# A planner's urge count started at one: context blocks behind every block of x from the first layer on

## What is computed

```python
x = first_block(x, ...)      # layer 0: pool + gated mixer, FFN; layer 1: NSA attention + retention, FFN
h, hc = x, ctx
for i in range(2):           # second_block; ctx_out is true for i = 0 alone
    m, mc = adaln(c, ada_w[i], ada_b[i]), adaln(c_ctx, ada_w[i], ada_b[i])
    h  = half_ffn(h,  m,  0, ..., ffn_w_in[i, 0], ffn_w_out[i, 0])
    hc = half_ffn(hc, mc, 0, ..., ffn_w_in[i, 0], ffn_w_out[i, 0])
    y, yc = mixer_i(modulated_norm(h), modulated_norm(hc), ...)  # i = 0: differential attention, i = 1: GQA
    h  = half_ffn(gated_residual(h, y), m, 6, ..., ffn_w_in[i, 1], ffn_w_out[i, 1])
    if ctx_out:
        hc = half_ffn(gated_residual(hc, yc), mc, 6, ...)
return h
```

## Time and profile before

| | us |
|---|---|
| median of 3 runs | 2725.43 |
| lowest, highest | 2722.52, 2730.79 |
| the profiled execution, its own time | 2730.84 |
| its span | 2729.1 |
| PE busy | 2536.8 (93%) |
| DVE busy | 1692.8 (62%) |
| ACT busy | 1246.3 (46%) |
| mean granted TensorE clock | 0.966 |
| loads | 480.11 MB, mean 176 GB/s |

### The profile page before, as it was taken

How to read it: one execution, slowest core, us unless ns; L and a number is a source line. 1 busy time by engine, 2 the same in 40 slices (tenths; PEclk the granted TensorE clock), 3 DMA queues, 4 the chain that set the end, 5 groups by cost and what they waited for, 6 DMA issues and landing times.

```text
span 2729.1 us, 48500 instructions
## 1 busy us (share of the span) xinstructions
PE 2536.8 (93%) x20604; PEld 2410.3 (88%) x20604; DVE 1692.8 (62%) x2817; ACT 1246.3 (46%) x1697; POOL 1.2 (0%) x6
## 2 busy tenths in 40 slices
PE   6799997999999999999898998999999999887998
PEld 5689986888998999999887998999999999766998
DVE  6565564656756655566767566577655557746655
ACT  4443452444544444445455454445444445435443
POOL 0000000000000000000000000000000000000000
PEclk9799999999999999999898999999999999888999
DMA  6456655523555665644351344554545545363453
GB/s 218 175 198 247 240 204 210 207 99 125 195 181 216 237 231 195 222 140 157 124 189 47 112 179 145 183 185 171 179 162 185 186 174 182 120 216 136 170 178 116
DMA packets 71590, 480.11 MB, mean 176 GB/s; under 512 B 8785, under 2 KB 9297, under 8 KB 17745
## 3 DMA queue, kind: packets, MB, share of 16 engines
q1 hardware_dynamic: 66240, 468.74, 48.1%
q10 hardware_dynamic: 5136, 8.28, 1.0%
HBM read 471.48 MB, written 1.05 MB: 173 GB/s over the span
## 4 chain that ended last, share of the span: by engine, by line
PE 75%; DVE 12%; ACT 6%; DMA 4%; issue 3%; ACTq 0%; DVEq 0%
PE bank L263 66%; ACT whi L222 3%; DMA raw<-w_main 2%; DVE wlo L242 2%; PE bank L1116 2%; DVE wlo L229 2%; PE bank L998 1%; PE bank L936 1%; DVE HX L638 1%; DVE ARX L687 1%; DVE tmpx L632 1%; DMA raw<-w_down 1%; PE bank L986 1%; PE bank L553 1%; PE bank L1640 0%
## 5 line engine op out<-in xcount | busy, mean ns | idle before, releaser
L263 PE MATMUL bank<-HNX_hi,whi 128*128 128x256 f32 x2968 | 865.9, 293 | 69.7 <-DVE wlo L242 28.3
L222 ACT ACTIVATE whi<-raw 128x2048 fp32r<-128x2048 f32 (+1 forms) x378 | 705.5, 1868 | 336.2 <-PE bank L263 168.2
L263 PE MATMUL bank<-HNX_hi,wlo 128*128 128x256 f32 x2968 | 849.6, 287 | 0.0
L263 PE MATMUL bank<-HNX_lo,whi 128*128 128x256 f32 x2968 | 835.2, 287 | 0.0
L229 DVE TENSOR_TENSOR wlo<-raw,whi 128x1024 fp32r<-128x1024 f32 (+1 forms) x378 | 453.5, 1200 | 575.1 <-ACT whi L222 574.6
L263 PEld LDWEIGHTS bank<-HNX_hi,whi 128*128 128x128 f32 x2968 | 582.0, 196 | 96.9 <-issue 52.0
L263 PEld LDWEIGHTS bank<-HNX_hi,wlo 128*128 128x128 f32 x2968 | 582.5, 196 | 0.0
L263 PEld LDWEIGHTS bank<-HNX_lo,whi 128*128 128x128 f32 x2968 | 574.0, 196 | 1.1 <-issue 0.9
L242 DVE TENSOR_TENSOR wlo<-raw,whi 128x1024 fp32r<-128x1024 f32 (+1 forms) x378 | 451.1, 1193 | 0.0
L263 PE MATMUL bank<-HNC_hi,whi 128*128 128x256 f32 x1344 | 389.0, 289 | 10.4 <-DVE HNC_lo L701 4.3
L263 PE MATMUL bank<-HNC_lo,whi 128*128 128x256 f32 x1344 | 380.7, 283 | 0.0
(11 more groups left out here) (341 smaller groups left out, 2945.4 us busy)
## 6 DMA issues: line engine op xcount, KB each, us to landing
raw<-w_main SPq DMA_DIRECT2D x270, 1024.0 KB, 4.8
raw<-w_ada SPq DMA_DIRECT2D x72, 1024.0 KB, 4.8
raw<-w_down SPq DMA_DIRECT2D x72, 1024.0 KB, 4.9
raw<-w_down SPq DMA_DIRECT2D x36, 768.0 KB, 4.2
raw<-w_cmp SPq DMA_DIRECT2D x4, 1024.0 KB, 5.1
tmpx<-ARX ACTq DMA_DIRECT2D x18, 128.0 KB, 4.6
tmpx<-ARX ACTq DMA_DIRECT2D x32, 64.0 KB, 4.7
HX<-x_in SPq DMA_DIRECT2D x2, 512.0 KB, 5.9
```

The source lines that it names most:

```text
L222: NS.activation(WHI[q % HIS][:, 0:size], RAW[m % SLOTS][:, 0:size], ACT.Copy).then_inc(sems["w_hi"], 1)
L263: return NT.matmul(dst, (WHI[ordinal[n] % HIS], WLO[n % SLOTS])[w][:, k * 2 * P + col:k * 2 * P + col + P], x[xp][:, kx, :], start=start, ...
```

## The change

One number: `urge[0]` starts at 1 instead of 0, so that `pace` may step c once before every half block of x from the start.

```diff
             lanes, ahead, paused = {}, {}, {"a"}
-            clock, ready_at, turns, urge = [0.0], {"c": 0.0, "a": 0.0}, [0], [0]
+            clock, ready_at, turns, urge = [0.0], {"c": 0.0, "a": 0.0}, [0], [1]
             DENSE, ADA = 2.9, 1.2
```

## The result

| | before | changed |
|---|---|---|
| median | 2723.97 us | 2776.08 us |
| lowest, highest | 2719.87, 2730.79 | 2773.81, 2779.39 |
| span of the profiled execution | 2729.1 | 2775.0 |
| mean granted TensorE clock | 0.966 | 0.955 |

The account below looks back on a forecast made before the run. PE, busy for 93% of the span, was taken as the bound, so only its own order could matter. Terms against the profiled execution summed to +5 us, 2736, or 2730 against the median of 2725.43; range 2706 to 2756.

Parts of the forecast that it names:

- The GQA: Keys and values of the GQA: x goes on earlier, c's two blocks and small steps only move; -11 us (-12 to -9).
- The norm before `gu2`: Five blocks of `da_in` become four of `da_out` with sums on DVE; 8 lost against 2.5, +6 us (0 to 11).
- `od_in`: Eight blocks of c spread over it: cover gains 4, the end of c's FFN costs 12; +8 us (-15 to +14).
- the differential attention: Nine units without a block for eight, the first three covered; +2 us (-3 to +6).
- the loop: NSA loop: 12 blocks of c for 18, units 0 to 4 bare, half of c's norm there; +8 us (3 to 15).
- Tail: NSA loop's end, tile norm to `od_out`: x's chain 17 us bare, taken as 22 with c's steps; +10 us (5 to 15).
- norm before `gu1`: From five blocks of c to none, with three of a and pieces of c's attention: 14 lost against 3.0, +11 (7 to 16).
- The norm before `gu4`: Two blocks of c for five, but these without sums or products on DVE; -2 us.
- `gu1` and `gu2`: The `gu1` term: 12 us of loss and small waits of about 3 leave, c's attention comes in; -13 us.
- Rival 1: More cover in `od_in` pays: that term becomes -22 for +8, giving 2700 us; chance 21%.
- Rival 2: NSA loop to `gu2`: lost cover costs full price, four terms 57 for 35, deciding past about 45; 2752 us, chance 24%.
- Rival 3: Lower clock in NSA's early units, its end and the norm, 0.74 instead of 1.00: +7, 2737 us; chance 11%.

Follow-up runs that it names:

- experiment 1: Kernel before, with the urge at 3 from x's `gu4` on, so c's two `ga_in` blocks and tile norm come earlier: 2710.12 us against 2726.52, ratio 0.9941.
- experiment 11: Kernel before, with the urge at 1 from the end of x's first FFN, so `od_in` has blocks of c without sums: 2744.19 us, ratio 1.0093.
- experiment 4: Kernel before, with c held during units 0 to 4 of the NSA loop: 2728.5 us, ratio 1.0008.
- experiment 7: Changed kernel, with the row of a finished ahead of the last two blocks of `od_in` instead of ahead of the NSA loop: 2772.92 us, ratio 1.0187.
- experiment 8: Changed kernel, with no row of a ahead of the NSA loop; a stops at a border of its rows: 2764.91 us, ratio 1.0159.
- experiment 10: Kernel before, with four blocks of a in a row ahead of its NSA loop, where it has one: 2734.63 us, ratio 1.0049.
- tail_bare: Kernel before, with c and a held from the end of the NSA loop to the norm (last of the 12 to 14 group): 2735.63 us, ratio 1.0048.
- experiment 3: Kernel before, with c held during x's norm before `gu1` alone: 2736.66 us, ratio 1.0034.
- experiment 6: Changed kernel, with the urge at 3 in x's `da_in` and back at 2 for the differential attention: 2768.94 us, ratio 1.0173.
- experiment 12: Changed kernel, with both c and a held from the end of the NSA loop to the end of the norm before `gu1`: 2763.0 us, ratio 1.0146.
- experiment 13: Kernel before, with c and a held during x's norm before `gu1` alone: 2730.86 us, ratio 1.0029.

## Why the prediction was wrong, step by step

**Right.** `gu0`, -1. The GQA, -13 for -11 (experiment 1). The norm before `gu2` and `da_in` within 4. `od_in`, +9 for +8, is right in what costs there, the end of c's FFN (experiment 11), and not in how: of its two parts the gain by cover was 2 and not 4, and the longest wait goes by ScalarE's order and not by VectorE's sums in a split. The five bare units cost 6 to 8 (experiment 4) for +8; that is partly luck, since the term had counted c's norm among them, and the run has no norm there.

With a's blocks and the small matmuls taken off, as in the prediction's norms, two terms broke out of their ranges most: the differential attention, +17 for +2 (upper end 6), and the loop, +18 for +8 (upper end 15). Tail and norm before `gu1`, +15 each, stand at or near their upper ends.

**"The three blocks of a ahead of it need no split and cost what they did."** This is the step that failed in kind. It counted them as PE work. In a row they empty the four buffers: 7 to 8 us in the loop (77.7 lost without their own work in the changed kernel, 69.7 and 71.0 when they stand elsewhere, experiments 7 and 8), 11 to 12 in the kernel before when put there (experiment 10). The prediction had reckoned with the four buffers in `od_in`, and did not ask the same of the loop's start. A second step failed in the same term: it took PE's work in the bare units at its covered price, 3.4 us for a unit. In the rows of the loop PE is idle for 12.7 us for 2.7, close to the term's 10 for 2, but 6.9 of them are the wait for the end of the row, which the term did not have. And PE's work itself got longer: its busy time, less 0.1195 for each matmul of a block and less a's 2.8, is 65.1 us for 56.4, at a granted clock of 0.90 for 0.99. So the loop's 21 are 10 of idle time, 9 of slower small matmuls and 3 of a's work.

**The tail**, +22 for +10 (upper end 15). x's bare chain was sized well: 18.3 us in the run `tail_bare` (VectorE's timeline, 663.33 to 681.59) for 17. With its guests it takes 25.4 in the changed kernel (831.60 to 857.00) for the 22 taken. What the term left out is the first block of `od_out`. The prediction said that it starts at the lower clock and gave that no price: its 48 matmuls take 9.5 us for 5.7, with pieces of c's attention between them, and 8.5 in the bare run, where the granted clock of the stretch is 0.64.

**The norm before `gu1`**, +20 for +11 (upper end 16). I took a middle between rows with pieces of the attention alone and with three blocks of a alone. By the measure of those rows the norm now loses 31.5 - 84 x 0.1195 - 3.2 = 18.3, nearly the 18.8 of the row with three blocks of a: that row and not the middle was the one to take. In the table's measure the bare price is 6 to 9 over before; each guest adds 9 to 14 to it. What I took for filling is a load on the chain; for a's blocks the trace of experiment 3 shows how, for the pieces of the attention it is not taken apart.

**The differential attention**, +19 for +2, the largest miss. The term said that the first three units are covered, by short blocks of c, and did not carry on to what these leave on VectorE: 16 sums, the residual and a half split in one piece, 9.85 us of PE's time (experiment 6). The price of such sums stood in the earlier trace rows and was charged in `od_in` only. Nor did it ask what stands beside x's tile norm at the end: before, blocks of c to the last; now none, a wait of 7.8 us. How much of the 19 each makes up was not isolated.

**The norm before `gu4`**, +7 for -2. Two blocks for five. In the run of experiment 6, which has none there, it loses 10.6; in the kernels with five, 4.7 to 9.8. No experiment isolates it.

**`gu1` and `gu2`**, -25 for -13. Part of c's attention is now in tail, `od_out` and norm, and is booked there.

**The rivals.** Rival 1, more cover in `od_in` pays, fell with experiment 11. Rival 2, cover that is gone costs its full price, named the right places, and its condition was met: the four terms with the tail pass 45 (21 + 22 + 20 + 10 = 73). Its ends were too low, since it left out the loads behind a and knew nothing of the differential attention. Rival 3, the clock: the mean granted clock fell from 0.966 to 0.955, which is 186 and 250 us at 1.2 GHz instead of 2.4; PE's busy time rose by 15.4 us, twice the 7 put down, and 9 of them in the NSA loop, one of its places. It is a part of the miss, not the whole: PE's idle time rose by twice as much. The Trainium skill, page "TensorE: Matmul & The Clock Gate", section "HAM oscillation — how this bites in real kernels", reckons such time as lost by half. An estimate by it, half of 64 us, is 32; the trace shows less, 15.4 at most.

## What to carry to other kernels

Ask of every piece of work that fills a gap what it holds besides its engine: a buffer and a load, and steps on the engines that the gap's own chain runs on. A piece with 1 us on TensorE and 1 MB to load is not a filler: three more in a row cost up to 17.6 us for 2.8 us of work. And when lanes are shifted against each other, follow the ends of their layers (sums, residual, norm), not only their blocks. Weigh a local price against the whole: in experiments 4, 6, 7 and 12 to 14 a stretch gained or lost 6 to 21 us, and most of it came back elsewhere.

## What the runs showed of the hardware

The order of ScalarE carries a delay to work that has nothing to do with it: rows of a ready since 684.6 were read at 691.1, behind two roundings that waited for DMA; in `od_in` the rounding of a block of x stood behind 8.04 us of wait for a residual of c. PE's named releaser in both is ScalarE or VectorE; the cause is one step behind it.

Lanes of different functions side by side make ScalarE load its function tables more often: 14 instructions more in the changed kernel (1711 for 1697), 55 such loads for 41, 18.0 of the 19.8 us by which it is busier. With c and a held out of tail and norm there are 47, so up to 8 of the 14 belong to c's attention there and the others to other places. In the changed kernel, from the tail to the norm before `gu1`:

```profile
L532 ACT ACT_TABLE_LOAD x3 | 3.8, 1283 | 0.1
L1868 ACT ACT_TABLE_LOAD x1 | 1.3, 1283 | 0.0
L1037 ACT ACT_TABLE_LOAD x1 | 1.3, 1283 | 0.0
L524 ACT ACT_TABLE_LOAD x1 | 1.3, 1283 | 0.0
```

With c and a held the same stretch has two such loads, of L532. The Trainium skill, page "ScalarE activation tables: per-element evaluation and per-set limits", section "What a function is on this engine", puts two functions of different sets one load of 1283 ns apart; the trace agrees, with 1283 ns as the mean of each of these rows.
